# Column groups, broadcast loads and an earlier row scaling in a hybrid decoder step

## The reference, cut to what matters

```python
x = x + y                                     # token mixer: gated conv and linear attention
x = x + mem_attend(rmsnorm(x, nmem), mk, mv, wq, wom)
x = x + hier_moe(rmsnorm(x, nf), ...)
...
def mem_attend(h, mk, mv, w_q, w_o):          # 4 heads of 256
    q = (h @ w_q).reshape(Bn, T, MEM_HEADS, MEM_DH)
    s = jnp.einsum('bthd,bmhd->bhtm', q, mk) * (MEM_DH ** -0.5)
    p = jax.nn.softmax(s, axis=-1)
    o = jnp.einsum('bhtm,bmhd->bthd', p, mv).reshape(Bn, T, D_MODEL)
    return o @ w_o
```

## Time and profile before

| | us |
|---|---|
| median of 3 runs | 1307.39 (1301.67 to 1308.06) |
| the profiled execution | 1304.67 |
| its span | 1302.6 |
| PE busy | 1137.8 (87%) |
| DVE busy | 645.6 (50%) |
| ACT busy | 482.4 (37%) |
| mean granted clock of PE | 0.933 |

### The profile page before, as it was taken

How to read it: one execution, slowest core, us unless ns; L and a number is a source line. 1 busy time by engine, 2 the same in 40 slices (tenths; PEclk the granted TensorE clock), 3 DMA queues, 4 the chain that set the end, 5 groups by cost and what they waited for, 6 DMA issues and landing times.

```text
span 1302.6 us, 16978 instructions
## 1 busy us (share of the span) xinstructions
PE 1137.8 (87%) x6470; PEld 969.7 (74%) x6471; DVE 645.6 (50%) x894; ACT 482.4 (37%) x752; POOL 65.3 (5%) x66
## 2 busy tenths in 40 slices
PE   5879988999999998899999999999845999999940
PEld 5866988889898888899886866779844666776620
DVE  2541440355444316555465532143467577677739
ACT  3552442221111025444532332243423555555513
POOL 1000000000000000000000000000001222222100
PEclk9998989999999899899999999999955999999985
DMA  7643111111113106567754524436755488589746
GB/s 192 185 144 102 49 33 33 33 33 33 33 33 86 49 33 216 141 175 198 226 174 118 178 81 149 151 100 182 217 194 196 145 292 278 187 273 377 273 181 268
DMA packets 191427, 196.79 MB, mean 151 GB/s; under 512 B 16106, under 2 KB 167930, under 8 KB 190076
## 3 DMA queue, kind: packets, MB, share of 16 engines
q1 hardware_dynamic: 184452, 178.99, 43.8%
q0 software_dynamic: 6912, 16.92, 3.6%
HBM read 170.30 MB, written 33.85 MB: 157 GB/s over the span
## 4 chain that ended last, share of the span: by engine, by line
PE 74%; DVE 12%; ACT 6%; issue 3%; DMA 3%; SPq 0%; DVEq 0%; POOLq 0%; ACTq 0%
PE G L1115 14%; PE G L1117 13%; PE G L1116 13%; PE G L668 6%; PE G L648 3%; PE G L650 3%; PE G L649 3%; PE G L1390 2%; PE T L1405 2%; PE T L1163 2%; PE G L1427 2%; ACT w_hi L1442 2%; DVE w_lo L1701 2%; DVE arena L1766 2%; PE T L637 1%
## 5 line engine op out<-in xcount | busy, mean ns | idle before, releaser
L1115 PE MATMUL G<-act_hi,w_hi 128*128 128x344 f32 (+4 forms) x1304 | 431.8, 331 | 23.6 <-DVE w_lo L1701 6.1
L1116 PE MATMUL G<-act_lo,w_hi 128*128 128x344 f32 (+4 forms) x1304 | 418.1, 321 | 0.0
L1117 PE MATMUL G<-act_hi,w_lo 128*128 128x344 f32 (+4 forms) x1304 | 417.9, 320 | 0.0
L1701 DVE TENSOR_TENSOR w_lo<-arena,w_hi 128x1024 fp32r<-128x1024 f32 (+1 forms) x113 | 137.3, 1215 | 312.6 <-ACT w_hi L1442 312.5
L1115 PEld LDWEIGHTS G<-act_hi,w_hi 128*128 128x128 f32 (+1 forms) x1304 | 249.6, 191 | 51.4 <-issue 36.3
L1116 PEld LDWEIGHTS G<-act_lo,w_hi 128*128 128x128 f32 (+1 forms) x1304 | 249.8, 192 | 3.0 <-issue 1.2
L1117 PEld LDWEIGHTS G<-act_hi,w_lo 128*128 128x128 f32 (+1 forms) x1304 | 248.9, 191 | 1.7
L1442 ACT CAST w_hi<-arena 128x1024 fp32r<-128x1024 f32 (+1 forms) x113 | 117.3, 1038 | 216.6 <-PE G L1117 191.0
L879 DVE TENSOR_TENSOR act_lo<-arena,act_hi 128x1024 fp32r<-128x1024 f32 x96 | 111.2, 1220 | 41.6 <-ACT act_hi L729 41.5
L729 ACT CAST act_hi<-arena 128x1024 fp32r x96 | 93.6, 1046 | 52.0 <-issue 44.3
L595 POOL DMA_INDIRECT arena<-d_h,tidx x24 | 37.3, 1556 | 1009.4 <-issue 995.1
(11 more groups left out here) (286 smaller groups left out, 1209.5 us busy)
## 6 DMA issues: line engine op xcount, KB each, us to landing
arena<-in_w_gate_dram SPq DMA_DIRECT2D x16, 1024.0 KB, 8.8
arena<-in_w_up_dram SPq DMA_DIRECT2D x16, 1024.0 KB, 12.0
arena<-in_w_down_dram SPq DMA_DIRECT2D x16, 1024.0 KB, 5.3
arena<-in_w_in_dram SPq DMA_DIRECT2D x24, 512.0 KB, 3.9
arena<-in_w_out_dram SPq DMA_DIRECT2D x24, 512.0 KB, 4.9
arena<-in_w_q_dram SPq DMA_DIRECT2D x24, 512.0 KB, 6.3
arena<-in_w_o_dram SPq DMA_DIRECT2D x24, 512.0 KB, 6.1
arena<-in_x_prompt_dram SPq DMA_DIRECT2D x16, 512.0 KB
```

Of the source, the lines that this page charges most:

```text
L1115: pe.matmul(out, a_hi, b_hi, start=first, stop=False)
L1116: pe.matmul(out, a_hi, b_lo, start=False, stop=False)
L1117: return pe.matmul(out, a_lo, b_hi, start=False, stop=last)
L1701: v.tensor_tensor(w_lo[:, n % 2, :, 0:width], raw[:, n % RAW, :, 0:width], w_hi[:, n % 2, :, 0:width], ALU.subtract).then_inc(s["split_don ...
```

## The change

Four edits. Value products: the four of one sample go to four groups of 32 partitions of one PSUM bank; `sout` copies that bank, and a product with a folding matrix adds the two memory halves where there was a transpose. Query rows: `qs` is stored to DRAM, and SP loads each row with one copy for every partition into one of two buffers; the selector, its products and their semaphore go. Key steps stand at other units: three in pass 4 and five in pass 5; the softmax and the value steps follow one unit later. Scaled rows: `nh` and `sp` stand ahead of a unit's entry, in a new list `ahead`, with the same unit.

```diff
+    ahead = {p: {u: [] for u in range(KB)} for p in range(len(PASSES))}
...
-            beside[p][2 * i + 1].append(("nh", j + i))
+            ahead[p][2 * i + 1].append(("nh", j + i))
...
-        beside[p][u + 1].append(("sp", i))
+        ahead[p][u + 1].append(("sp", i))
...
-    KEYS = [(4, 1), (4, 3), (4, 4), (4, 6), (4, 7), (5, 0), (5, 1), (5, 3)]
-    VALS = [(5, 7), (6, 0), (6, 1), (6, 2), (6, 3), (6, 4), (6, 5), (6, 6)]
+    KEYS = [(4, 3), (4, 5), (4, 6), (5, 0), (5, 1), (5, 3), (5, 4), (5, 5)]
+    VALS = [(6, 0), (6, 1), (6, 2), (6, 3), (6, 4), (6, 5), (6, 6), (6, 7)]
...
-    beside[4][2].append(("gain3", 0))
-    beside[5][5].append(("smax", 0))
-    beside[5][6].append(("sprob", 0))
+    beside[4][1].append(("qstore", 0))
+    beside[4][2] += [("qload", 0), ("qload", 1)]
+    beside[5][6].append(("gain3", 0))
+    beside[5][6].append(("smax", 0))
+    beside[5][7].append(("sprob", 0))
...
         for b in range(KB):
+            order += ahead[p][b]
             order.append(("unit", at[(kind, (c, b))]))
...
+            def load_query(b):
+                sp.dma_start(qrow[b % 2], d_qs[b].partition_broadcast(P)).then_inc(s[f"qb_in{b % 2}"], 16)
...
                     if i >= 2:
-                        sp.wait_ge(s["q_sc"], 2 * i - 2)
+                        sp.wait_ge(s["q_sc"], i - 1)
+                        load_query(i)
...
+                elif what == "qstore":
+                    sp.wait_ge(s["q_ev"], 1)
+                    sp.dma_start(d_qs, qs).then_inc(s["q_st"], 16)
...
-                        ins = pe.transpose(T[:, 0, k * DB * MH:(k + 1) * DB * MH], so[:, k * P:(k + 1) * P],
-                                           ident[0:DB * MH, 0:DB * MH])
+                        ins = pe.matmul(T[:, 0, k * DB * MH:(k + 1) * DB * MH], so[:, (k % 4) * P:(k % 4 + 1) * P],
+                                        fold[:, k // 4, :], start=True, stop=True)
...
-                        pe.matmul(back[:, c, :], sel_a[:, i, :], qs[:, c * 512:(c + 1) * 512], start=True,
-                                  stop=True).then_inc(s["q_bc"], 1)
...
-                            ins = pe.matmul(back[0:DB * MH, c, :], pTz[:, m, i, :], cache[i % 2][:, m, c * 512:(c + 1) * 512],
-                                            start=(i == 0 and m == 0), stop=(i == DB - 1 and m == MB - 1))
+                            r0 = (2 * c + m) * DB * MH
+                            ins = pe.matmul(back[r0:r0 + DB * MH, 0, :], pTz[:, m, i, :], cache[i % 2][:, m, c * 512:(c + 1) * 512],
+                                            start=(i == 0), stop=(i == DB - 1))
...
-                    act.copy(so.rearrange("p (a n) -> p a n", a=2), back[0:DB * MH]).then_inc(s["so_ev"], 1)
+                    act.copy(so, back[:, 0, :]).then_inc(s["so_ev"], 1)
...
-                    v.tensor_copy(sel_a, bcast(ident[0:DB, 0:DB].unsqueeze(2), [DB, DB, P])).then_inc(s["q_ev"], 1)
...
-                                                             in1=back[:, c, j * DH:(j + 1) * DH], scale=1.0, scalar=0.0,
+                                                         in1=qrow[i % 2][:, h * DH:(h + 1) * DH], scale=1.0, scalar=0.0,
```

More of the change, by code:

```diff
@@ L239, in build @@
         d_h3 = dram("d_h3", [COLS, D])
+        d_qs = dram("d_qs", [DB, D])
         d_y = dram("d_y", [2 * COLS, D])
@@ L300, in build @@
         sel_g = region("tmp", 0, DB * P, DB).rearrange("q (b p) -> q b p", b=DB)
-        sel_a = region("qe", D, DB * P, DB).rearrange("q (b p) -> q b p", b=DB)
+        qrow = [region("qe", i * D, D) for i in range(2)]
         qs = region("S", 0, D, DB)
@@ L308, in build @@
         pTz = region("vtm", KB * MEM + MB * D, MB * DB * DB * MH).rearrange("p (m b e) -> p m b e", m=MB, b=DB)
-        so = region("S", 0, D, DB * MH)
+        so = region("S", 0, 512)
         HT = SEQ // 2
@@ L345, in build @@
         mk_in mv_in s_mm s_mx s_e s_p s_tr s_pT s_pvhi
-        kc_in0 kc_in1 vc_in0 vc_in1 q_tr q_ev q_bc q_sc q_t2 q_mx q_ex q_pn q_t3 q_pT q_o q_ohi q_olo
+        kc_in0 kc_in1 vc_in0 vc_in1 q_tr q_ev q_st qb_in0 qb_in1 q_sc q_t2 q_mx q_ex q_pn q_t3 q_pT q_o q_ohi q_olo
         r_mm r_L r_ge r_gexp r_d r_dexp r_M r_rank r_slot r_tab iota_rdy l_tr l_ids
@@ L417, in build @@
         csrow = region("tmp", 2 * TW, CONV, 2 + DB)
+        fold = sb("fold", [P, 2, DB * MH])
         uend = sb("uend", [P, CB, 2 + DB])
@@ L1066, in _ @@
                     if i < 2:
-                        sp.wait_ge(s["q_sc"], 2 * DB - (2 if i == 0 else 0))
+                        sp.wait_ge(s["q_sc"], DB - 1 + i)
                     else:
@@ L1070, in _ @@
                     sp.dma_start(cache[i % 2], cache_mem_v[0, i].rearrange("(m p) h d -> p m (h d)", p=P)).then_inc(s[f"vc_in{i % 2}"], 16)
+                elif what == "qstore":
+                    sp.wait_ge(s["q_ev"], 1)
+                    sp.dma_start(d_qs, qs).then_inc(s["q_st"], 16)
+                elif what == "qload":
+                    if i == 0:
+                        sp.wait_ge(s["h_done"], 2 * TILES)
+                        sp.wait_ge(s["q_st"], 16)
+                    load_query(i)
                 elif what == "gain3":
-                    sp.wait_ge(s["h_done"], 2 * TILES)
+                    sp.wait_ge(s["q_sc"], DB)
                     sp.dma_start(gain, norm_ffn[0].partition_broadcast(P)).then_inc(s["gain_in"], 16)
@@ L1358, in _ @@
                 elif what == "smax":
-                    pe.wait_ge(s["q_sc"], 2 * DB)
+                    pe.wait_ge(s["q_sc"], DB)
                     for m in range(MB):
@@ L1908, in _ @@
                     y_lo(i[0], i[1])
-                elif what == "sq":
-                    v.tensor_copy(sel_a, bcast(ident[0:DB, 0:DB].unsqueeze(2), [DB, DB, P])).then_inc(s["q_ev"], 1)
                 elif what == "smax":
-                    dve.wait_ge(s["q_sc"], 2 * DB)
+                    dve.wait_ge(s["q_sc"], DB)
                     link(v.memset(pTz, 0.0))
+                    e = DB * MH
+                    link(v.tensor_tensor(fold[:, :, :], ident[:, :].rearrange("p (c m e) -> p c m e", c=2, m=2)[:, :, 0, :],
+                                         ident[:, :].rearrange("p (c m e) -> p c m e", c=2, m=2)[:, :, 1, :], ALU.add))
                     dve.wait_ge(s["q_t2"], 1)
@@ L1927, in _ @@
                     if i >= 1:
-                        dve.wait_ge(s["q_sc"], 2 * i)
+                        dve.wait_ge(s["q_sc"], i)
                     dve.wait_ge(s[f"kc_in{i % 2}"], 16 * (i // 2 + 1))
[L1930 to L1937, removed]
-                                                             in1=back[:, c, j * DH:(j + 1) * DH], scale=1.0, scalar=0.0,
[L1939 to L1943, removed]
+                    dve.wait_ge(s[f"qb_in{i % 2}"], 16 * (i // 2 + 1))
+                    for m in range(MB):
+                        for h in range(MH):
+                            ins = v.tensor_tensor_reduce(out=kprod, in0=cache[i % 2][:, m, h * DH:(h + 1) * DH],
+                                                         in1=qrow[i % 2][:, h * DH:(h + 1) * DH], scale=1.0, scalar=0.0,
+                                                         op0=ALU.mult, op1=ALU.add,
+                                                         accum_out=ksc[:, m, i * MH + h:i * MH + h + 1])
+                            if not (m == MB - 1 and h == MH - 1):
+                                link(ins)
+                    ins.then_inc(s["q_sc"], 1)
                 elif what == "sc":
```

## The result

The changed kernel takes 1258.80 us (median of 4 runs, 1258.26 to 1264.93), the kernel before 1307.72 (4 runs beside it, 1301.67 to 1311.92): ratio 0.9632, 95% interval 0.9599 to 0.9664. Run once more it took 1260.39 (median of 6) against 1305.47, ratio 0.9662 (0.9632 to 0.9692). Forecast were 1262 us and a range of 1252 to 1282. The profiled execution of the changed kernel took 1258.85 us, its span 1256.8, against 1304.67 and 1302.6.

What follows compares the result with a forecast made beforehand. TensorE work was taken as the bound, 74% of the chain of waits. Gains of 15.6 - 0.9 + 20.4 + 5.5 + 1.4 + 2.7 + 0.4 = 45.1 us took 1304.67 to 1259.6, 1262 as a median; range 1252 to 1282.

Steps and rivals of the forecast that it cites:

- Query broadcasts: Passes 4 and 5: eight row broadcasts leave TensorE, replaced by broadcast loads; 1.95 us each, 15.6 us gained.
- the walk: Step-by-step schedule of passes 4 and 5: loads land in 8 to 10 us, TensorE stands 2.4 and 2.0 us.
- the slower rival (D): Passes 4 and 5: broadcast loads land late, later keys wait on DVE and TensorE stops; about 1311 us; chance 0.03.
- Spread of keys: Passes 4 and 5: old key stall gains 0.3 us, new stand at the score transposes loses 2.0; together about -0.9 us.
- Value products: Sample value products: four column groups work at once, 3.55 us per sample becomes 1.0; 20.4 us saved over eight.
- Rivals A and B: On the value products: A, column groups run one after another, 1282, chance 0.11; B, half overlap in order, 1272, chance 0.08.
- Scaled rows ahead: Row scaling before the weight split shortens TensorE stalls: 5.5 us in pass 1, 1.4 in pass 3, 2.7 in passes 7 and 8.
- rival E: Scaled rows did not hold TensorE, weights land late: passes 1, 7, 8 give 1 us, not 8.2; 1269; chance 0.04.
- Small terms: Sample output copy has half the columns, 0.4 us gained; selector copy goes, small DVE addition comes, both beside TensorE.

## Why the prediction was right, point by point

- **Query broadcasts, 15.6 us.** Right in the mechanism, 1.2 us too small: 16.8 by the run that put them back. The forecast read 1.91 us off and added "about 0.1" for the units that now adjoin, then took 1.95. The neighbours of those rows show more:

```profile
650.75 0.34 PE L1117 MATMUL G<-act_hi,w_lo 128*128 128x384 f32 x1
...
653.20 0.34 PE L1116 MATMUL G<-act_lo,w_hi 128*128 128x384 f32 x1
```

  From one to the other are 2.45 us, where two records on in a dense run take 0.35: the broadcast cost 2.10 us. The loads land in 4.4 us (5.4 at most), not the 8 to 10 of the walk, so the slower rival (D) had no ground at all.
- **Spread of keys, -0.9 us.** The two stands of the walk came as drawn: 2.41 us at the attention value products (forecast 2.4), 2.02 at the scores (2.0), none for the probabilities. What it left out is a third, the 0.73 us behind ScalarE's copy just ahead of the first (the last line of the waits above). 5.2 us of standing against 3.5 before make -1.7, and the stretch of the table leaves -1.5 (15.3 less 16.8). These rows of the changed kernel show the first, key 2, split and subtraction in a row on DVE:

```profile
678.38 0.42 DVE L1945 CUSTOM_DVE_ANT_0 arena<-arena 128x256 f32<-128x256 f32 x1
...
678.73 1.22 DVE L1712 TENSOR_TENSOR w_lo<-arena,w_hi 128x1024 fp32r<-128x1024 f32 x1
...
679.87 0.75 DVE L1965 TENSOR_TENSOR act_lo<-G,act_hi 128x256 fp32r<-128x256 f32 x2
...
680.34 0.92 PE L1438 MATMUL G<-arena 128*128 128x256 f32 x3 [2.41 <-DVE act_lo L1965]
```

  What the walk did not see is that a second cause lay just behind the first: with the key away, the weight load for ScalarE gives a stand of the same length. And leaving more keys in pass 4 would have cost 3.9 us by (6,0), more than the walk's balance of under a microsecond suggests.
- **Value products, 20.4 us.** Right to 0.1 us: 2.55 a sample. The row of the quarter-array products of the linear attention was the right one to size it by; the runs with one, two and four groups give 3.55, 1.85 and 1.00 us, which is 8, 4 and 2 records of 0.43 us and 0.11 to 0.14 for entry. Rivals A and B are out. The Trainium skill, "TensorE: Matmul & The Clock Gate", section "Part 3: Packing small matmuls", gives 2.38 times for three column groups; four give 3.55 times here, and its line that weight loads overlap running products only where the row groups differ does not hold in this trace: the eight weight loads of one sample, all of the same 128 rows, take 0.16 us together, inside the 0.62 us of the first four records (start us, us, as above).

```profile
803.66 0.16 PEld L1401 LDWEIGHTS G<-arena 128*32 128x32 f32 x8 [0.24 <-issue]
```

- **Scaled rows ahead, 5.5 + 1.4 + 2.7 us.** Right: 5.6, 1.5 and 3.0, and undoing it alone gives pass 1 and pass 3 back to 0.1 us (rival E is out). The 1.5 us that should remain in pass 1 are 1.64, with the full clock behind them; in the repeat only 0.4 us remain. That the row scaling of the probabilities moves at no cost was not tried by itself. Pass 3 gave most back to the loop over SP's queue, and breaking that loop won 4.7 us.
- **Small terms, +0.4 us.** Wrong in sign: -0.8. I counted the smaller copy and left out that the fold takes two records per product and 16 in all: 1.81 us against 0.61. It failed because a new instruction was costed at nothing for being of the same number as the old.
- **The sum.** 45.1 us forecast; from the end of the early stage to the last unit's copy 44.9 were measured, and 46.8 in the repeat. That the first agrees to 0.2 us is luck: the broadcasts gave 1.2 us more than forecast, the spread of keys 0.6 less and the small terms 1.2 less, the scaled rows 0.5 more. The agreement of the whole time (1262 against 1258.8 and 1260.4) is no finer than the 6 us by which single executions differ.

## What to carry to other kernels

Small products that share their rows can be spread over column groups of TensorE and then cost the longest group's records; look for a row of the same trace in which part of the array works in parallel, and size by it. Before work is taken off an engine, walk the other engines' queues through the faster schedule: here that gave two stands to a tenth of a microsecond and missed a third of 0.73 us. A stand behind one late step often has a second cause just as late; moving the first only (a key, a softmax) moved or kept the stand, and only the order in SP's queue took one away.

## Not expected of the hardware

The granted clock behind a short stand (1.00 is 2.4 GHz all along, a mean below it holds time at 1.2 GHz) is not the same from one execution to the next. Behind the attention value products of pass 4, one code gave these two stretches (the changed kernel, then its repeat):

```profile
680.40:690.00 9.60, 9.44 (x36) 7.52 (x37) 2.77 (x7) 2.24 (x6) 0.00 (x0) 0.82 0.88 282
```
```profile
684.10:693.70 9.60, 9.38 (x46) 7.68 (x45) 2.54 (x6) 2.23 (x6) 0.00 (x0) 1.00 0.88 277
```

The stands ahead of them were 2.41 and 2.33 us, each behind one of 0.73, and the first execution lost 1.4 us by it. The first stand of pass 3 was 2.13 us in the changed kernel with 1.00 behind it, and 2.17 us in the run with two column groups with 0.82 behind it:

```profile
617.40:627.00 9.60, 7.67 (x64) 7.45 (x64) 5.81 (x6) 4.90 (x8) 0.00 (x0) 1.00 0.58 155
```
```profile
616.70:626.00 9.30, 9.30 (x64) 9.12 (x64) 5.53 (x6) 4.75 (x8) 0.00 (x0) 0.82 0.60 159
```

In pass 1 the clock stayed at 1.00 behind 1.6 us in the five executions that had this stand, and fell behind 4.1 us in the two that had that one. But a shorter stand is not safe for that: behind the 1.05 us ahead of the fold it was 1.00 in the changed kernel and 0.81 in the run with scores a unit later (1.06 us), where 1.6 us more were lost by (7,0):

```profile
817.00:826.00 9.00, 9.00 (x62) 8.96 (x62) 2.25 (x6) 1.82 (x6) 0.00 (x0) 1.00 0.01 2
```
```profile
821.00:830.00 9.00, 9.00 (x52) 8.96 (x53) 0.54 (x5) 1.60 (x6) 0.00 (x0) 0.81 0.01 2
```

A stand of 1 to 2.5 us costs its length or, where TensorE sets the pace behind it, some 1.5 us more; what decides between the two stays open. The forecast's choice that 1.5 us keep the full clock held in pass 1, but these runs do not make it a rule.
